# One more stage in the pipeline of latent attention, and two groups of loads sent later

## The chip, the cores and the metric

One core of a Trainium2 chip runs the whole kernel. The time is that of one execution on the device, in microseconds (us), and the median of several runs is compared. Smaller is better.

## The reference

The kernel is one inference step of a two-layer streaming encoder for 576 tokens: 512 of a prompt (SEQ) and 64 of a stream that is continued (DEC), which has a cache of 256 past keys. Both have a width of 1024 (D). Each layer is a half-step feed-forward (width 2816), a mixer, and a second half-step feed-forward. Every sub-layer is modulated by a conditioning vector c and followed by a LayerNorm:

```python
mod = (silu(c) @ w_ada[l] + b_ada[l]).reshape(B, 3, 3, 1, D_MODEL)
shift, scale, gate = mod[:, :, 0], mod[:, :, 1], 1.0 + mod[:, :, 2]
h = swiglu(x * (1.0 + scale[:, 0]) + shift[:, 0], w_ff_in[l, 0], w_ff_out[l, 0])
x = layer_norm(DEEP_ALPHA * x + 0.5 * gate[:, 0] * h, ln_g[l, 0], ln_b[l, 0])
```

The first layer's mixer holds four gated-delta heads and four heads of latent attention, side by side. The attention is this, in blocks of 128 queries, with keys visible by chunks of 64:

```python
s = (einsum('bqhd,bkhd->bhqk', q_nope, k_nope) + einsum('bqhr,bkr->bhqk', q_rope, k_rope)) * MLA_SCALE
p = softmax(where(visible, s, -inf), axis=-1)
out = einsum('bhqk,bkhd->bqhd', p, v)
```

All is in float32. The second layer's mixer is a diagonal state-space layer.

## The kernel before, in words

**The whole.** Each engine has its own program, and semaphores (s_...) order them. TensorE (PE) multiplies tiles of 128 features by 288 tokens. A float32 product is made of three products of rounded parts (hi by hi, hi by lo, lo by hi; `three`, L268). Weights come in blocks of 1 MB or less through a ring of three buffers on SyncE's (SP) DMA queue (`stream_load`, L244); ScalarE (ACT) makes the hi part of a block (`split_hi`, L252) and VectorE (DVE) the lo part (`split_lo`, L259). Activations are split in the same way: ACT makes u_f and u_hi (L538, L542), GpSimd (POOL) makes u_lo (L563).

**The start.** Three DMA queues are issued at once. SP: c_col, c_act (both forms of the conditioning vector), then in turn four pieces each of ada_w0 and ada_w1 (1 MB each; the first rows of the modulation weights), then the weight blocks of the first feed-forward. ACT: x (2304 KB), then nine constants, masks (448 KB) and swap (192 KB) the third and fourth of them. POOL: two pieces of 1 MB of ada_w, the modulation weights for the later rows, whose products DVE makes between blocks of the first feed-forward (`ada_unit`, L655). The order of `ada_vector_first` (L679) is: after the silu of c_act (s_ada_c), sixteen products of ada_w1 (two for each of eight tiles, counted in s_mod1), then a wait for all constants (s_cst), then for PE's sum over ada_w0 (`ada_tensor_first`, L665; s_mod0), then the bias, u_scale and u_shift. ACT splits weight blocks 0 and 1 and then modulates x; PE begins the feed-forward (`head`, L321 on, through `half_step`, L280) when a block's lo part and the first u_lo are there.

masks is read by the gated-delta scan (from 657.9 us on), swap by four products of L1622 that turn the rotary parts (861.3 us).

**Latent attention.** It goes over 20 units: four query blocks by four heads, with 128, 256, 384 and 512 keys, then four decode units of 64 queries and 320 keys. For unit n:

- PE, scores: L1634 and L1635 write one bank of PSUM, bank n % 2.
- DVE: for prompt units the mask (L1729), the row maximum (L1730) and its negative (L1731; s_mx).
- ACT: the exponential into pp, with the row sum (L1686; s_sx).
- DVE: reciprocal and normalising of pp (L1737, L1738; s_pn).
- PE: transpose of pp, 128 keys at a time (L1658; s_tp).
- ACT: copy into ppt (L1696, L1698; s_pc).
- PE: product with the values vt (L1647; s_pv). Every four units ACT and DVE take the hi and lo part of the result (L1704, L1744; s_oh, s_ol).

Each engine has one loop over n, written out by hand. Iteration n holds on PE: scores of n, three matmuls whose result nobody reads (`keep_warm`, L291, in iterations 0 to 9), values of n-2, transpose of n-1. On ACT: exponential of n, copy of n-1. On DVE: maximum of n, then normalising of n-1. After the last unit PE waits for s_ol and begins the output projection (mix_out, L273).

Of the kernel before, what the change touches and what calls it, by code (L numbers as in the profile page):

```python
# [19 lines left out]
ALU = mybir.AluOpType  # L20
# [67 lines left out]
N_CONST = 9 + 1  # L88
# [24 lines left out]
def trunk(nc, i, o):  # L113
# [86 lines left out]
    s_ada_c = sem("conditioning_ready")  # L200
    s_ada_t = sem("modulation_tile_summed")
# [580 lines left out]
    ck_hi, ck_lo = (rt3(n, [P, KPAD], F32R) for n in ("ck_hi", "ck_lo"))  # L782
    rtmp = rt3("rtmp", [P, TOKENS])
    pp = rt3("pp", [P, 2, 512])
# [522 lines left out]
    def gdn_vector(dve):  # L1307
# [71 lines left out]

        dve.wait_ge(s_blk, g_mla)  # L1380
# [195 lines left out]
    NU = len(UNITS)  # L1576

# [10 lines left out]
    def mla_tensor(pe):  # L1588
# [29 lines left out]
        pe.wait_ge(s_evac, g_mla + 2)  # L1618
        for n_, (w, src) in enumerate(((swap[:, 0, :], qr[:, 0, :]), (swap[:, 0, :], qr[:, 1, :]),
                                       (swap[0:64, 1, :], misc[0:64, :]), (swap[0:64, 2, :], misc[0:64, :]))):  # L1620
            for a in range(2):
                mm = pe.matmul(pair(n_)[:, a, :], w, halves(src)[:, a, :], start=True, stop=True)  # L1622
            mm.then_inc(s_rp, 1)
# [3 lines left out]
        for n in range(NU + 2):  # L1627
            if n < NU:
                h, q0, nq, k0, nk = UNITS[n]
                p0 = (h % 2) * 64  # L1630
                if n >= 2:
                    pe.wait_ge(s_sx, n - 1)
                out = ps[0:nq, n % 2, 0:nk]
# [3 lines left out]
            if n < 10:  # L1637
                keep_warm(pe, 6, 3)
            if 2 <= n:
                u = n - 2  # L1640
                h, q0, nq, k0, nk = UNITS[u]
# [8 lines left out]
            if 1 <= n <= NU:  # L1650
                u = n - 1
                h, q0, nq, k0, nk = UNITS[u]
                pe.wait_ge(s_pn, u + 1)
                if u >= 2:
                    pe.wait_ge(s_pc, u - 1)
                for t in range(-(-nk // P)):
                    w = min(P, nk - t * P)
                    mm = pe.transpose(ps[0:w, 2 + u % 2, t * P:t * P + nq], pp[0:nq, u % 2, t * P:t * P + w],  # L1658
                                      ident[0:nq, 0:nq])
                mm.then_inc(s_tp, 1)  # L1660

    def mla_scalar(act):
# [17 lines left out]
        for n in range(NU + 2):  # L1680
            if n < NU:
                h, q0, nq, k0, nk = UNITS[n]
                act.wait_ge(s_mx, n + 1)
                if n >= 2:
                    act.wait_ge(s_tp, n - 1)
                act.activation(pp[0:nq, n % 2, 0:nk], ps[0:nq, n % 2, 0:nk], ACT.Exp, bias=sm[0:nq, 1, n:n + 1],  # L1686
                               scale=MLA_SCALE, accum_out=sm[0:nq, 2, n:n + 1]).then_inc(s_sx, 1)
            if 1 <= n <= NU:
                u = n - 1
# [10 lines left out]
            if n >= 2 and n % 4 == 1:  # L1700
                h, q0, nq, k0, nk = UNITS[n - 2]
                gi = (n - 2) // 4
                act.wait_ge(s_pv, n - 1)
# [4 lines left out]
    def mla_vector(dve):  # L1708
# [14 lines left out]
        for n in range(NU + 2):  # L1723
            if n < NU:
                h, q0, nq, k0, nk = UNITS[n]
                dve.wait_ge(s_sc, n + 1)
                if q0 < SEQ:

                    link(dve.memset(ps[0:CH, n % 2, nk - CH:nk], -1e30))  # L1729
                link(dve.tensor_reduce(sm[0:nq, 0, n:n + 1], ps[0:nq, n % 2, 0:nk], AX.X, ALU.max))  # L1730
                dve.tensor_scalar(sm[0:nq, 1, n:n + 1], sm[0:nq, 0, n:n + 1], -MLA_SCALE, None,  # L1731
                                  ALU.mult).then_inc(s_mx, 1)
            if 1 <= n <= NU:
# [4 lines left out]
                dve.tensor_scalar(pp[0:nq, u % 2, 0:nk], pp[0:nq, u % 2, 0:nk], sm[0:nq, 3, u:u + 1], None,  # L1738
                                  ALU.mult).then_inc(s_pn, 1)
            if n >= 2 and n % 4 == 1:  # L1740
                h, q0, nq, k0, nk = UNITS[n - 2]
                gi = (n - 2) // 4
# [529 lines left out]
    def s5_tensor(pe):  # L2272
# [102 lines left out]
        for b in range(1, 4):  # L2375
            product(pe, "glu", b, 2, KD, u_hi, u_lo)
        out_tensor(pe, "s5_out", 4, KD, glu_hi, lambda k: h_lo[:, k, :], lambda k: pe.wait_ge(s_gl, k + 1))
    constant_loads = [(ident[:, :], i["ident"]), (mean_w[:, :], i["mean_w"]), (masks[:, :, :], i["masks"]),
                      (swap[:, :, :], i["swap"]), (onecol[:, :], i["onecol"]), (b_ada[:, :, :], i["b_ada"]),
                      (ln_g[:, :, :], i["ln_g"]), (ln_b[:, :, :], i["ln_b"]), (cols[:, :], i["cols"])]  # L2380
# [16 lines left out]
    def _(pool):  # L2397
        ada_load(pool, 0, UNITS0, 0)
        u_gpsimd(pool, 0)
# [203 lines left out]
```

## Time and profile before

| | |
|---|---|
| median of 3 runs | 2555.35 us (2549.14 to 2561.02) |
| profiled execution | 2571.54 us, its span 2569.9 us |
| PE busy | 2466.7 us, 96% of the span |
| DVE, ACT, POOL busy | 1453.2, 722.2, 142.5 us |
| mean granted TensorE clock | 0.980 |
| HBM read, written | 259.13 MB, 13.32 MB |

Busy time of PE is the sum of its matmul records, whose ends are modelled. A granted clock of 1.00 is 2.4 GHz, 0.50 is 1.2 GHz. The profiled execution is a single one, 16 us above the median of the timed runs, so differences are worked out within it and then set against the median.

### The profile page before, as it was taken

To read this page: it belongs to the slowest core of one execution; us is meant where nothing else is said; L and a number is where in the kernel's file an instruction comes from. 1 tells how busy PE (TensorE), PEld (TensorE's weight loads), DVE (VectorE), ACT (ScalarE), POOL (GpSimd) and SP (SyncE) were. 2 spreads that over 40 slices of the span, in tenths; PEclk is the share of its full clock that TensorE was granted. 3 is DMA by queue.
4 is the path that set the end of the run, shared out by engine and by line. 5 is a ranking of instruction groups with operands and counts; after the bars stand their busy time and mean duration, and the time that the engine had idled before them with its cause. 6 is when DMAs were issued, how large, how long until landed. Compare 5 with 4: busy or idle time off the path is not lost.

```text
span 2569.9 us, 41177 instructions
## 1 busy us (share of the span) xinstructions
PE 2466.7 (96%) x18104; PEld 2366.9 (92%) x18104; DVE 1453.2 (57%) x2311; ACT 722.2 (28%) x1002; POOL 142.5 (6%) x215
## 2 busy tenths in 40 slices
PE   6999999999899989999999999999989999999996
PEld 6999999998787668999999999999968989999995
DVE  4767765574563435864465686677667455333323
ACT  3211121444333324311121521221255243111212
POOL 2000000200000001100000200000000010000001
PEclk9999999999997889999999999999989999999998
DMA  6445542122000012443343154333324122222221
GB/s 281 150 161 185 183 166 96 64 90 49 13 1 17 27 66 74 159 162 116 122 164 121 61 180 156 111 144 145 140 74 138 58 74 83 78 83 86 83 72 48
DMA packets 55873, 275.09 MB, mean 107 GB/s; under 512 B 7216, under 2 KB 17008, under 8 KB 33040
## 3 DMA queue, kind: packets, MB, share of 16 engines
q1 hardware_dynamic: 38304, 177.43, 19.7%
q0 software_dynamic: 15952, 91.73, 10.1%
q8 instruction: 142, 2.33, 0.4%
q10 hardware_dynamic: 1440, 3.32, 0.4%
q14 instruction: 35, 0.29, 0.0%
HBM read 259.13 MB, written 13.32 MB: 106 GB/s over the span
## 4 chain that ended last, share of the span: by engine, by line
PE 66%; DVE 5%; ACT 1%; issue 1%; DMA 0%; POOL 0%; SPq 0%; DVEq 0%; ACTq 0%
PE ps L273 50%; PE ps L280 4%; PE ps L497 2%; PE ps L480 2%; DVE x L599 1%; PE ps L291 1%; PE ps L1200 1%; PE ps L1209 1%; DVE ln_rstd_tail L595 1%; PE ps L1635 1%; PE ps L1213 0%; PE ps L2338 0%; PE ps L1429 0%; PE ps L1634 0%; PE ps L1420 0%
## 5 line engine op out<-in xcount | busy, mean ns | idle before, releaser
L273 PE MATMUL ps<-u_hi,w_hi 128*128 128x288 f32 x3040 | 653.2, 296 | 2.1 <-DVE w_lo L265 1.2
L273 PE MATMUL ps<-u_hi,w_lo 128*128 128x288 f32 x3040 | 650.3, 296 | 0.0
L273 PE MATMUL ps<-u_lo,w_hi 128*128 128x288 f32 x3040 | 650.3, 296 | 0.0
L265 DVE TENSOR_TENSOR w_lo<-w_raw,w_hi 128x2048 fp32r<-128x2048 f32 (+3 forms) x184 | 360.6, 1960 | 350.0 <-ACT w_hi L257 346.3
L257 ACT ACTIVATE w_hi<-w_raw 128x2048 fp32r<-128x2048 f32 (+3 forms) x184 | 303.5, 1649 | 888.8 <-DMA w_raw<-in_w_in 420.1
L273 PEld LDWEIGHTS ps<-u_hi,w_hi 128*128 128x128 f32 x3040 | 490.7, 189 | 6.8 <-issue 3.5
L273 PEld LDWEIGHTS ps<-u_lo,w_hi 128*128 128x128 f32 x3040 | 490.5, 189 | 0.0
L273 PEld LDWEIGHTS ps<-u_hi,w_lo 128*128 128x128 f32 x3040 | 490.1, 189 | 0.0
L621 DVE SCALAR_TENSOR_TENSOR ada_out<-ada_w,c_act 128x1024 f32<-128x1024 f32 x272 | 317.0, 1221 | 28.8 <-DMA ada_w<-in_w_ada 26.9
L273 PE MATMUL ps<-h_lo,w_hi 128*128 128x288 f32 x1392 | 293.4, 295 | 0.0
L273 PE MATMUL ps<-h_hi,w_hi 128*128 128x288 f32 x1296 | 280.9, 298 | 0.0
L273 PE MATMUL ps<-h_hi,w_lo 128*128 128x288 f32 x1296 | 276.7, 295 | 0.0
L423 DVE TENSOR_TENSOR hf<-ps,sg 128x576 f32<-128x576 f32 x88 | 66.6, 757 | 305.3 <-ACT sg L406 305.3
L273 PEld LDWEIGHTS ps<-h_lo,w_hi 128*128 128x128 f32 x1392 | 222.3, 188 | 0.0
L273 PEld LDWEIGHTS ps<-h_hi,w_hi 128*128 128x128 f32 x1296 | 209.6, 188 | 2.1
L273 PEld LDWEIGHTS ps<-h_hi,w_lo 128*128 128x128 f32 x1296 | 208.3, 188 | 0.0
L406 ACT ACTIVATE sg<-ps 128x576 f32<-128x576 f32 x88 | 57.2, 650 | 491.5 <-PE ps L273 483.1
L449 DVE SCALAR_TENSOR_TENSOR x<-ps,res_gate,x 128x224 f32<-128x224 f32 (+2 forms) x240 | 85.9, 412 | 109.7 <-PE ps L273 85.7
L280 PE MATMUL ps<-u_hi,w_hi 128*128 128x288 f32 x352 | 109.0, 310 | 7.9 <-POOL u_lo L563 7.9
L280 PE MATMUL ps<-u_lo,w_hi 128*128 128x288 f32 x352 | 104.5, 297 | 0.0
L280 PE MATMUL ps<-u_hi,w_lo 128*128 128x288 f32 x352 | 104.3, 296 | 0.0
L563 POOL TENSOR_TENSOR u_lo<-u_f,u_hi 128x288 fp32r<-128x288 f32 x80 | 70.9, 901 | 432.8 <-ACT u_hi L542 431.0
(384 smaller groups left out, 2604.0 us busy)
## 6 DMA issues: line engine op xcount, KB each, us to landing
w_raw<-in_w_in SPq DMA_DIRECT2D x88, 1024.0 KB, 4.8
ada_w<-in_w_ada POOLq DMA_DIRECT2D x64, 1024.0 KB, 4.9
w_raw<-in_w_out SPq DMA_DIRECT2D x32, 768.0 KB, 4.4
w_raw<-in_w_out SPq DMA_DIRECT2D x32, 640.0 KB, 3.8
w_raw<-in_w_mix_in SPq DMA_DIRECT2D x10, 1024.0 KB, 4.9
ada_w<-in_w_ada SPq DMA_DIRECT2D x8, 1024.0 KB, 26.1
output_matrices<-wm_new POOLq DMA_DIRECT2D x8, 576.0 KB, 3.1
wm<-output_matrices POOLq DMA_DIRECT2D x8, 576.0 KB, 4.4
```

What stands on the lines that cost most here:

```text
L257: act.activation(w_hi[:, g % NS, 0:WIDTH[g]], w_raw[:, g % NS, 0:WIDTH[g]], ACT.Copy).then_inc(s_whi, 1)
L265: dve.tensor_tensor(w_lo[:, g % NS, 0:WIDTH[g]], w_raw[:, g % NS, 0:WIDTH[g]], w_hi[:, g % NS, 0:WIDTH[g]].bitcast(F32), ALU.subtract).the ...
L273: m = pe.matmul(out[:, a, :], w, mv[:, a, :], start=start and n_ == 0, stop=stop and n_ == 2)
L280: m = pe.matmul(out, w, mv, start=start and n_ == 0, stop=stop and n_ == 2)
L291: pe.matmul(ps[:, bank_, :], w[:, 0:P], w[:, P:P + 512], start=True, stop=True)
L406: act.activation(halves(sg[:, b % 2, :]), pair(2 * (b % 2)), ACT.Silu).then_inc(s_sg, 1)
L423: dve.tensor_tensor(halves(hf[:, b % 2, :]), pair(2 * (b % 2) + 1), halves(sg[:, b % 2, :]), ALU.mult).then_inc(s_evac, 1)
L449: return dve.scalar_tensor_tensor(out=x[:, b, lo:hi], in0=pair(2 * (b % 2))[:, a, lo - a * HALF:hi - a * HALF], scalar=res_gate[:, site, b ...
L480: return pe.matmul(pair(1)[:, a, :], mean_w[:, :], half(x, k, a), start=k == 0, stop=k == KD - 1)
L497: pe.matmul(pair(3)[:, a, :], mean_w[:, :], sq[:, k % SQ, :], start=k == 0, stop=k == KD - 1).then_inc(s_var, 1)
L563: pool.tensor_tensor(half(u_lo, k, a), half(u_f32, k, a), half(u_hi, k, a).bitcast(F32), ALU.subtract).then_inc(s_up, 1)
L621: return dve.scalar_tensor_tensor(out=ada_out[:, n % 2, :], in0=w, scalar=1.0, in1=c_act[:, st, :], op0=ALU.mult, op1=ALU.mult, accum_out= ...
```

## The change

1. **Loads at the start.** masks and swap leave ACT's list of constants (nine become seven, so s_cst counts eight loads with x). POOL first waits until DVE has made 14 of the sixteen products of ada_w1, then issues its first two pieces of ada_w and after them masks and swap, which count on a semaphore of their own, s_late. DVE waits for s_late before the scan, PE before L1622.
2. **The attention loop.** Scores go through three banks (0, 1 and 6) and pp has three buffers; the first of them lies on rtmp's place, which is no longer needed then. PE's iteration n is now: scores of n, warming matmuls, transpose of n-2, values of n-3. ACT copies n-2; DVE still normalises n-1. The loops have one more iteration, and the u_hi and u_lo pairs move one iteration later.
3. **Warming matmuls.** Two in iterations 0 to 7, in bank 7, in place of three in iterations 0 to 9, in bank 6.

```diff
-N_CONST = 9 + 1
+N_CONST = 7 + 1
...
+    PP0 = rt3.at
     rtmp = rt3("rtmp", [P, TOKENS])
-    pp = rt3("pp", [P, 2, 512])
+    rt3.at = PP0
+    pp = rt3("pp", [P, 3, 512])
...
+        dve.wait_ge(s_late, 32)
         dve.wait_ge(s_blk, g_mla)
...
+    SCORE_BANK = (0, 1, 6)
+    def score(n, rows_, a, b):
+        return ps[0:rows_, SCORE_BANK[n % 3], a:b]
...
+        pe.wait_ge(s_late, 32)
...
-        for n in range(NU + 2):
+        for n in range(NU + 3):
             if n < NU:
-                if n >= 2:
-                    pe.wait_ge(s_sx, n - 1)
-                out = ps[0:nq, n % 2, 0:nk]
+                if n >= 3:
+                    pe.wait_ge(s_sx, n - 2)
+                out = score(n, nq, 0, nk)
...
-            if n < 10:
-                keep_warm(pe, 6, 3)
-            if 2 <= n:
+            if n < 8:
+                keep_warm(pe, 7, 2)
+            if 2 <= n < NU + 2:
                 u = n - 2
+                h, q0, nq, k0, nk = UNITS[u]
+                pe.wait_ge(s_pn, u + 1)
+                if u >= 2:
+                    pe.wait_ge(s_pc, u - 1)
+                for t in range(-(-nk // P)):
+                    w = min(P, nk - t * P)
+                    mm = pe.transpose(ps[0:w, 2 + u % 2, t * P:t * P + nq], pp[0:nq, u % 3, t * P:t * P + w],
+                                      ident[0:nq, 0:nq])
+                mm.then_inc(s_tp, 1)
+            if n >= 3:
+                u = n - 3
                 h, q0, nq, k0, nk = UNITS[u]
                 pe.wait_ge(s_pc, u + 1)
...
-            if 1 <= n <= NU:
-                u = n - 1
-                h, q0, nq, k0, nk = UNITS[u]
-                pe.wait_ge(s_pn, u + 1)
...
-                if n >= 2:
-                    act.wait_ge(s_tp, n - 1)
-                act.activation(pp[0:nq, n % 2, 0:nk], ps[0:nq, n % 2, 0:nk], ACT.Exp, bias=sm[0:nq, 1, n:n + 1],
+                if n >= 3:
+                    act.wait_ge(s_tp, n - 2)
+                act.activation(pp[0:nq, n % 3, 0:nk], score(n, nq, 0, nk), ACT.Exp, bias=sm[0:nq, 1, n:n + 1],
                                scale=MLA_SCALE, accum_out=sm[0:nq, 2, n:n + 1]).then_inc(s_sx, 1)
-            if 1 <= n <= NU:
-                u = n - 1
+            if 2 <= n < NU + 2:
+                u = n - 2
...
-            if n >= 2 and n % 4 == 1:
+            if n >= 3 and n % 4 == 2:
...
-    constant_loads = [(ident[:, :], i["ident"]), (mean_w[:, :], i["mean_w"]), (masks[:, :, :], i["masks"]),
-                      (swap[:, :, :], i["swap"]), (onecol[:, :], i["onecol"]), (b_ada[:, :, :], i["b_ada"]),
-                      (ln_g[:, :, :], i["ln_g"]), (ln_b[:, :, :], i["ln_b"]), (cols[:, :], i["cols"])]
+    constant_loads = [(ident[:, :], i["ident"]), (mean_w[:, :], i["mean_w"]), (onecol[:, :], i["onecol"]),
+                      (b_ada[:, :, :], i["b_ada"]), (ln_g[:, :, :], i["ln_g"]), (ln_b[:, :, :], i["ln_b"]),
+                      (cols[:, :], i["cols"])]
...
     def _(pool):
+        pool.wait_ge(s_mod1, 2 * KD - 2)
         ada_load(pool, 0, UNITS0, 0)
+        pool.dma_start(masks[:, :, :], i["masks"]).then_inc(s_late, 16)
+        pool.dma_start(swap[:, :, :], i["swap"]).then_inc(s_late, 16)
         u_gpsimd(pool, 0)
```

## Rows read from the trace of the kernel before

**Rows 1.** Page, part 4: shares of the chain that ended last, by engine.
```profile
...
PE 66%; DVE 5%; ACT 1%; issue 1%; DMA 0%; POOL 0%; SPq 0%; DVEq 0%; ACTq 0%
...
```

**Rows 2.** Timeline, 0 to 52 us: start us, us, engine, line, operation [idle before <-releaser].
```profile
...
1.41 1.22 POOL L648 DMA_DIRECT2D ada_w<-in_w_ada  x2 [0.83 <-POOLq L2595]
...
15.29 1.89 ACT L637 ACTIVATE c_act<-c_act 128x2048 f32<-128x2048 f32 x1
...
20.11 27.44 PE L671 MATMUL ps<-c_col,ada_w 128*128 128x2 f32 x128 [20.11 <-DMA ada_w<-in_w_ada]
...
40.88 1.23 DVE L621 SCALAR_TENSOR_TENSOR ada_out<-ada_w,c_act 128x1024 f32<-128x1024 f32 x1 [1.67 <-DMA ada_w<-in_w_ada]
...
45.91 1.91 ACT L257 ACTIVATE w_hi<-w_raw 128x2048 fp32r<-128x2048 f32 x1 [0.56 <-DMA w_raw<-in_w_in]
47.69 0.17 DVE L677 TENSOR_TENSOR mod<-ps,b_ada_sb 128x16 f32<-128x16 f32 x1 [2.13 <-PE ps L671]
...
51.54 0.58 PE L280 MATMUL ps<-u_hi,w_hi 128*128 128x288 f32 x1 [3.98 <-POOL u_lo L563]
...
```

**Rows 3.** DMA queues, 0 to 20 us: packets, MB, share of 16 engines.
```profile
...
q0 software_dynamic: 288, 2.10, 24.9%
...
```

**Rows 4.** Windows: us, PE, PEld, DVE, ACT, POOL busy, PEclk, DMA share, GB/s.
```profile
...
16.00:20.00 4.00, 0.00 (x0) 0.00 (x0) 0.00 (x0) 1.18 (x1) 0.00 (x0) 1.00 1.02 424
...
```

**Rows 5.** DMA issues, 0 to 90 us: queue, count, KB each, us to landing.
```profile
...
masks<-in_masks ACTq DMA_DIRECT2D x1, 448.0 KB, 22.6
...
```

**Rows 6.** Timeline of TensorE in latent attention.
```profile
...
870.57 0.49 PE L1634 MATMUL ps<-kn,qn 128*128 128x128 f32 x2 [1.28 <-DVE kr L1722]
...
886.17 0.60 PE L1634 MATMUL ps<-kn,qn 128*128 128x256 f32 x2
...
887.32 0.97 PE L291 MATMUL ps<-w_hi 128*128 128x512 f32 x3
888.13 0.60 PE L1647 MATMUL ps<-ppt,vt 128*128 128x128 f32 x4
...
919.04 0.66 PE L1658 MATMUL ps<-ident,pp 128*128 128x128 f32 x4 [0.67 <-DVE pp L1738]
919.53 1.02 PE L1634 MATMUL ps<-kn,qn 128*128 128x512 f32 x2
...
921.54 1.16 PE L1647 MATMUL ps<-ppt,vt 128*128 128x128 f32 x8
923.36 0.66 PE L1658 MATMUL ps<-ident,pp 128*128 128x128 f32 x4 [0.67 <-DVE pp L1738]
923.95 0.75 PE L1634 MATMUL ps<-kn,qn 128*64 128x320 f32 x2
...
925.31 1.16 PE L1647 MATMUL ps<-ppt,vt 128*128 128x128 f32 x8
...
942.91 0.85 PE L273 MATMUL ps<-u_hi,w_hi 128*128 128x288 f32 x2 [0.93 <-DVE u_lo L1744]
...
```

**Rows 7.** Timelines of VectorE, then ScalarE, for one unit of 512 keys.
```profile
...
921.69 0.11 DVE L1729 MEMSET ps<- 64x64 f32 x1 [2.71 <-PE ps L1635]
...
922.82 0.49 DVE L1738 TENSOR_SCALAR pp<-pp,sm 128x512 f32<-128x512 f32 x1
...
922.75 0.69 ACT L1686 ACTIVATE pp<-ps,sm 128x512 f32<-128x512 f32 x1 [2.42 <-DVE sm L1731]
...
924.05 0.60 ACT L1696 ACTIVATE ppt<-ps 128x512 f32<-128x512 f32 x1 [0.53 <-PE ps L1658]
...
```

**Rows 8.** Waits, 870 to 942 us: waiter <- releaser: us in total, times, longest.
```profile
...
PE ps L1658 <- DVE pp L1738: 6.6, 13, 0.9
...
```

**Rows 9.** Windows in latent attention; columns as in rows 4.
```profile
...
870.50:882.00 11.50, 11.44 (x40) 8.36 (x41) 3.37 (x20) 2.66 (x11) 0.54 (x1) 0.70 0.06 14
898.00:915.00 17.00, 13.51 (x61) 7.30 (x60) 7.14 (x25) 6.02 (x15) 0.00 (x0) 1.00 0.00 1
935.00:942.00 7.00, 6.05 (x25) 4.81 (x24) 1.61 (x6) 1.37 (x6) 0.00 (x0) 0.50 0.01 2
...
```

More of the change, by code:

```diff
@@ L200, in trunk @@
     s_ada_c = sem("conditioning_ready")
+    s_late = sem("late_constants_loaded")
     s_ada_t = sem("modulation_tile_summed")
@@ L1649, in mla_tensor @@
                 mm.then_inc(s_pv, 1)
-            if 1 <= n <= NU:
-                u = n - 1
-                h, q0, nq, k0, nk = UNITS[u]
-                pe.wait_ge(s_pn, u + 1)
[L1654 to L1660, printed above, removed]
     def mla_scalar(act):
@@ L1679, in mla_scalar @@
         split_hi(act, g_mla + 3)
-        for n in range(NU + 2):
+        for n in range(NU + 3):
             if n < NU:
@@ L1699, in mla_scalar @@
                 ins.then_inc(s_pc, 1)
-            if n >= 2 and n % 4 == 1:
-                h, q0, nq, k0, nk = UNITS[n - 2]
-                gi = (n - 2) // 4
-                act.wait_ge(s_pv, n - 1)
+            if n >= 3 and n % 4 == 2:
+                h, q0, nq, k0, nk = UNITS[n - 3]
+                gi = (n - 3) // 4
+                act.wait_ge(s_pv, n - 2)
                 act.activation(u_hi[:, 4:8, q0:q0 + nq],
@@ L1722, in mla_vector @@
         dve.tensor_tensor(kr[:, 0:TOKENS], kr[:, 0:TOKENS], rtmp[:, :], ALU.add).then_inc(s_kr, 1)
-        for n in range(NU + 2):
+        for n in range(NU + 3):
             if n < NU:
@@ L1727, in mla_vector @@
                 if q0 < SEQ:
-                    link(dve.memset(ps[0:CH, n % 2, nk - CH:nk], -1e30))
-                link(dve.tensor_reduce(sm[0:nq, 0, n:n + 1], ps[0:nq, n % 2, 0:nk], AX.X, ALU.max))
+                    link(dve.memset(score(n, CH, nk - CH, nk), -1e30))
+                link(dve.tensor_reduce(sm[0:nq, 0, n:n + 1], score(n, nq, 0, nk), AX.X, ALU.max))
                 dve.tensor_scalar(sm[0:nq, 1, n:n + 1], sm[0:nq, 0, n:n + 1], -MLA_SCALE, None,
@@ L1737, in mla_vector @@
                 link(dve.reciprocal(sm[0:nq, 3, u:u + 1], sm[0:nq, 2, u:u + 1]))
-                dve.tensor_scalar(pp[0:nq, u % 2, 0:nk], pp[0:nq, u % 2, 0:nk], sm[0:nq, 3, u:u + 1], None,
+                dve.tensor_scalar(pp[0:nq, u % 3, 0:nk], pp[0:nq, u % 3, 0:nk], sm[0:nq, 3, u:u + 1], None,
                                   ALU.mult).then_inc(s_pn, 1)
-            if n >= 2 and n % 4 == 1:
-                h, q0, nq, k0, nk = UNITS[n - 2]
-                gi = (n - 2) // 4
+            if n >= 3 and n % 4 == 2:
+                h, q0, nq, k0, nk = UNITS[n - 3]
+                gi = (n - 3) // 4
                 dve.wait_ge(s_oh, 4 + gi + 1)
```

## The prediction

> **What bounds the kernel now.** I read the page first: the chain of work that ended last is 66% TensorE (PE) [rows 1], and elsewhere it jumps between engines. So a change pays where PE starts late or waits. I looked for PE's idle time in the two stretches that the diff touches, with the timeline, the DMA queues, the waits and the granted clock.
>
> *The start.* In [rows 2] PE's first instruction is the 128-column product of L671 at 20.11 us, released by the first piece of ada_w0. From there it runs 27.44 us without a gap: 214 ns for each of 128 matmuls, a rate that later pieces don't hold up. VectorE (DVE) waits for its end at 47.69, modulates, splits the first weight block, and the first real matmul (L280) starts at 51.54. Before 20 us PE only waits for bytes: the DMA engines are full (share 1.02, 424 GB/s) [rows 4], and of what they moved by then 2.10 MB belongs to POOL's queue [rows 3]. Those are the two ada_w pieces issued at 1.41, which the FFN's first blocks use, after 64 us.
>
> *Latent attention.* The first score matmul is at 870.57, the first matmul of mix_out at 942.91 [rows 6]: 72.34 us for 20 units. In a unit of 512 keys the loop is closed through DVE: transposes of the last unit start at 919.04, scores at 919.53, the value product at 921.54; meanwhile DVE masks and takes the maximum from 921.69, and only then normalises the unit before, 922.82 to 923.31 [rows 7]; the next transpose starts at 923.36 [rows 6]. That is 4.32 us, with PE idle 0.67 us by the record and a little more, because a matmul's recorded end runs past the start of one that could follow. Over the stage this wait is 6.6 us in 13 places [rows 8]. ScalarE (ACT) is not the limit: exponential and copy take 0.69 and 0.60 us of the 4.32 [rows 7].
>
> **The change at the start.** POOL's first two loads (2.10 MB) and the masks and swap constants (0.46 and 0.20 MB; [rows 5] has the larger) now go out only after the 14th of DVE's sixteen modulation products. On a full DMA 2.10 MB take 2.10/0.42 = 5.0 us. All of it lies ahead of PE's start; the two constants mostly landed after it (masks 22.6 us after issue), so they relieve later pieces only. PE's start moves from 20.1 to 15.1. The silu of c_act, the other condition, ended at 15.29 + 1.89 = 17.18 [rows 2]; c_act is queued ahead of ada_w0 on SP and also comes earlier, since POOL's queue was sharing with it. A piece of 1.05 MB needs 2.5 us on a free DMA, so c_act lands near 12.5 and its silu ends near 14.5: enough, with little to spare. The 27.44 us follow, so DVE's bias step, and all behind it, come 5.0 us earlier.
>
> What is late next? The last ada_w1 piece, at 40.88 before, now lands some 2.75/0.42 = 6.6 us earlier, at 34.3; two products of 1.2 us later, near 36.7, POOL issues its four transfers (about 1.2 us for the first two [rows 2]; its next task, u_lo, is 8 us off). Weight block 0, next on SP's queue, has landed 2.5 us after that piece, at 36.8. Block 1 (45.91 before) would land at 39.3 alone. ACT splits it (1.91 us) before it may modulate, and modulation can start at 43.3, so block 1 has 2.1 us of slack. If POOL's data halve its rate for its last microsecond or two it is 1 to 2 us late: hidden. If all 2.10 MB went ahead of it, it would be 5.0 late, 2.9 on the path. The new waits on the late constants (DVE before the scan at 650 us, PE before L1622) have been met for hundreds of microseconds: nothing. Start: **-5.0 us**, bounds -2 (that collision) and -6.6 (every deferred byte counts).
>
> The Trainium skill ("DMA: Bandwidth & Descriptors", Queues, rings and completion order) says that each DMA engine goes round the queues packet by packet. By that rule block 1 gets half the rate while POOL's data flow, at worst 2.5 us late, 0.4 on the path; no row shows that collision.
>
> **The change in latent attention.** Per iteration PE did scores n, values n-2, transpose n-1; now it does scores n, transpose n-2, values n-3. Normalising n-2 is finished an iteration earlier, so the transpose waits for nothing; scores n needs the exponential of n-3; the value product needs a copy that ACT made one iteration before. One more iteration drains the pipe. So PE alone sets the pace, and I add its work, start to start [rows 6]:
> - scores: 512 keys 2.01 (919.53 to 921.54), 256 keys 1.15 (886.17 to 887.32), decode 1.36; 384 and 128 by the same slope 1.58 and 0.72. Four each: 27.3.
> - transposes: 0.49 for four tiles, 0.12 a tile, 52 tiles: 6.4.
> - values: four records busy 0.60, eight 1.16, so 0.14 a record, 104 records: 14.6.
> - warming matmuls: three take 0.81; now 2 in 8 iterations, 16 of 0.27 instead of 30: 4.3.
>
> Sum 52.6 us at full clock. To this come: the slow stretch at the front, where 11.5 us had a mean grant of 0.70 [rows 9], that is 6.9 us at half speed, in which PE work takes nearly twice its time: 3.3. The drain, where the last unit's exponential, normalisation, two copies and the u_hi/u_lo pair are exposed: 1.5. And a slow end: before, all of 935 to 942 was at 0.50 (1.2 GHz) [rows 9], with the end-to-end value products at 1.2 GHz; I take 2, between 0 (the clock holds) and 4 (all of the last units). Together 59.4, against 72.34: **-12.9 us**. Half of the gain comes out of waits, 4 us out of fewer warming matmuls. Bounds: -9, if moving between score, transpose and value products costs 0.2 us a unit that the rows hide; -17, if both slow stretches shrink.
>
> Do ACT and DVE keep pace? DVE's work for a unit of 512 keys ran from 921.69 to 923.31, 1.6 us; ACT's is 0.69 and 0.60 and a short readout between them [rows 7]. PE's new period is 3.6. The u_hi and u_lo of each fourth unit follow the value product of n-3 and stand on ACT and DVE ahead of the next maximum; they run beside the next score product, and PE doesn't take that unit's transpose until two iterations on. All of it is covered; uncovered, the pair would cost about one pass of 0.7 us four times.
>
> The edit most open to attack is the smaller number of warming matmuls. In [rows 9] PE had no such matmuls from 898 to 915, was busy 13.51 of 17.00 us, and kept a grant of 1.00; the new loop is denser than that. So I give the removal no price. The Trainium skill ("TensorE: Matmul & The Clock Gate", The HAM clock gate) says the opposite default: throttled unless activity releases it. Taken alone it would keep the front of the stage at 1.2 GHz; the row at 898 speaks against it for the rest.
>
> **Sum.** 5.0 + 12.9 = 17.9 us. The profiled execution took 2571.54 (span 2569.9), so it becomes 2553.6; the timed runs have a median 16 us lower, 2555.35, and from it the same saving gives **2537.4 us**, 0.7% less. A difference under 0.5%, 12.8 us, is about what a measurement can't tell from none.
>
> **Rivals.**
> - *Only the start pays* (0.10). The waits on DVE turn into waits on ACT: exponential, copy and u_hi in one queue. For: the chain touches all of them. Against: ACT's 1.5 us or so per unit [rows 7]. Then attention gives only the warming matmuls and a few waits, 5 us: 2545.
> - *Only attention pays* (0.07). PE's start is set by c_act and its silu, or by x ahead of it on the other queue, or block 1 is late: start -1 to -2, total 14: 2541.
> - *Both clocks hold* (0.10). No slow end in attention and none at the start of mix_out: 22 to 25 us, 2531.
> - *The clock falls and stays down* (0.04), the one that ends slower. With 14 fewer warming matmuls the front of the attention never gets back to 2.4 GHz. Each microsecond of the loop spent at half clock costs 0.4 to 0.5 us; 18 us of gain are eaten by 40 more slow microseconds, and if all 52.6 us of work run slow it is +23 - 18 + 3 = 8 us slower: 2563. For: the clock did fall at the front. Against: the same loop, less dense, held it at 898.
> - *The change does nothing at either place* (0.02): 2555.
> - The forecast itself (0.67): 2531 to 2543 for its own bounds.
>
> Range 2527 to 2547 us: it leaves out the slow-clock case, part of the case of only the start, and some scatter of the median on either side. Faster by over 0.5% needs 12.8 us: forecast, held clocks and most of the second rival, less scatter, 0.80; within 0.5%: 0.16; slower 0.04.
>
> **What the changed profile would show.** PE's L671 group starts near 15 and still lasts 27.4 us; the first L280 matmul starts near 46.5; DVE finds block 0 split; ACT's second split ends before 43. If block 1 is late, ACT's u_f follows that split directly. In attention the transposes wait for nothing on DVE, periods at 512 keys are 3.5 to 3.6 us, and the stage lasts 59 us. I am wrong if PE's idle before the transposes is replaced by idle before value products or scores (ACT as releaser), if PE's first start stays after 18 us, or if the granted clock is at 0.5 for more than some 15 us of the stage.

## The result, and the profile after

| | before | after |
|---|---|---|
| median of 11 runs | 2553.81 us | 2533.02 us |
| lowest to highest | 2535.28 to 2561.69 | 2517.7 to 2544.32 |
| ratio, 95% interval | | 0.9923, 0.9899 to 0.9946 |
| profiled execution, its span | 2571.54, 2569.9 us | 2528.1, 2526.4 us |

By the ratio the change saves 19.7 us (13.8 to 25.8); forecast were 17.9. The whole interval lies beyond 0.5%. Ratios here are those of the fast executions alone: in the session of the first four experiments five of 35 executions of the kernel before (2571 to 8041 us) and one of loop_warm30 (4827 us) are left out of them.

The two spans differ by 43.5 us, over twice what the medians do, so a difference of two profiles must be split before it is read. By the starts of the stages: the first feed-forward begins 5.2 us earlier; from there to the first product of the gated-delta scan 4.0 us are given back; from the scan to the attention it is 11.7 us less, because before had 27.3 us of it at a granted clock of 0.50, from 804.6 us on (before_again, the same kernel profiled once more, lacks that stretch and takes 9.9 us less there); the attention is 19.7 us shorter; the last feed-forward and what follows it are 10.7 us shorter, without an edit there (last section); the rest is 0.2. Only the first and the fourth answer to the edits.

The page after: busy time of each engine, the chain of work that ended last, and the DMA issues of ada_w on SP's queue.

```profile
...
PE 2435.6 (96%) x18090; PEld 2343.1 (93%) x18090; DVE 1453.6 (58%) x2311; ACT 719.6 (28%) x1002; POOL 143.6 (6%) x217
...
PE 66%; DVE 5%; ACT 1%; issue 1%; DMA 0%; POOL 0%; SPq 0%; DVEq 0%; ACTq 0%
...
ada_w<-in_w_ada SPq DMA_DIRECT2D x8, 1024.0 KB, 20.3
...
```

The shares of the chain are those of [rows 1]: the page doesn't show a gain of 0.8%. The stages do. First the start, as a timeline like [rows 2]:

```profile
...
12.22 1.89 ACT L638 ACTIVATE c_act<-c_act 128x2048 f32<-128x2048 f32 x1
...
14.95 27.44 PE L672 MATMUL ps<-c_col,ada_w 128*128 128x2 f32 x128 [14.95 <-DMA ada_w<-in_w_ada]
...
33.01 1.23 DVE L622 SCALAR_TENSOR_TENSOR ada_out<-ada_w,c_act 128x1024 f32<-128x1024 f32 x1 [0.36 <-DMA ada_w<-in_w_ada]
...
35.69 1.22 POOL L649 DMA_DIRECT2D ada_w<-in_w_ada  x2 [35.11 <-DVE ada_out L622]
...
39.52 1.91 ACT L258 ACTIVATE w_hi<-w_raw 128x2048 fp32r<-128x2048 f32 x1 [0.56 <-DMA w_raw<-in_w_in]
42.52 0.17 DVE L678 TENSOR_TENSOR mod<-ps,b_ada_sb 128x16 f32<-128x16 f32 x1 [4.84 <-PE ps L672]
...
46.37 0.58 PE L281 MATMUL ps<-u_hi,w_hi 128*128 128x288 f32 x1 [3.98 <-POOL u_lo L564]
...
```

PE's first product lasts 27.44 us as before and starts at 14.95, not 20.11. DVE's bias step follows at 42.52 (was 47.69), the first real matmul at 46.37 (was 51.54): each 5.2 us earlier. The split of block 1 starts at 39.52 and is over at 41.43, before the bias step. The idle time of DVE ahead of that step has grown from 2.13 to 4.84 us: DVE has more slack and PE alone sets the start. That the 5 us hold further on shows at the tail of the first feed-forward: its first product on L281 comes at 460.51, on L280 before at 465.64.

TensorE's timeline in the attention, the counterpart of [rows 6]:

```profile
...
857.67 0.49 PE L1644 MATMUL ps<-kn,qn 128*128 128x128 f32 x2 [1.25 <-DVE kr L1732]
...
884.77 1.02 PE L1644 MATMUL ps<-kn,qn 128*128 128x512 f32 x2
...
887.16 0.83 PE L1668 MATMUL ps<-ppt,vt 128*128 128x128 f32 x6
887.83 1.02 PE L1644 MATMUL ps<-kn,qn 128*128 128x512 f32 x2
...
891.00 1.02 PE L1644 MATMUL ps<-kn,qn 128*128 128x512 f32 x2
891.96 1.12 PE L1645 MATMUL ps<-kr,qr 64*128 64x512 f32 x2
893.01 0.66 PE L1657 MATMUL ps<-ident,pp 128*128 128x128 f32 x4
893.50 1.06 PE L1668 MATMUL ps<-ppt,vt 128*128 128x128 f32 x8
894.49 0.75 PE L1644 MATMUL ps<-kn,qn 128*64 128x320 f32 x2
...
907.18 2.23 PE L1668 MATMUL ps<-ppt,vt 128*128 128x64 f32 x12
910.34 0.85 PE L274 MATMUL ps<-u_hi,w_hi 128*128 128x288 f32 x2 [0.93 <-DVE u_lo L1754]
...
```

An iteration now mixes three units, so its length depends on all three. One iteration has scores, transposes and value products of 512 keys alone: 891.00 to 894.49, 3.49 us, against 4.32 for the same work before. (884.77 to 887.83 is 3.06 us, but its transposes and values are of 384 keys.) No transpose has a wait in brackets. The stage lasts 857.67 to 910.34, 52.67 us, against 72.34. The waits of the stage (columns as in [rows 8]) say the same: the line of 6.6 us in 13 places is gone, and what is left on PE inside the stage is its first wait, here with the two largest waits of the other engines, of which DVE's is for PE:

```profile
...
ACT pp L1696 <- DVE sm L1741: 35.4, 20, 8.7
...
DVE ps L1739 <- PE ps L1645: 11.7, 13, 1.5
...
PE ps L1644 <- DVE kr L1732: 1.2, 1, 1.2
...
```

ACT's wait for the maximum is long, but nothing on PE waits for ACT.

Three windows, columns as in [rows 4]: the front, the middle and the last units.

```profile
...
857.50:869.00 11.50, 11.33 (x51) 7.62 (x52) 5.72 (x31) 3.63 (x16) 0.54 (x1) 1.00 0.07 14
...
885.00:902.00 17.00, 17.00 (x83) 9.09 (x82) 8.27 (x26) 7.45 (x19) 0.00 (x0) 1.00 0.01 1
...
903.00:910.00 7.00, 6.37 (x38) 4.42 (x37) 2.43 (x8) 2.89 (x13) 0.00 (x0) 0.91 0.00 1
...
```

PE is busy for 17.00 of 17 us in the middle, and the granted clock is 1.00 at the front, where it was 0.70 [rows 9], and 0.91 at the end, where it was 0.50: it fell at 908.7 us, 1.6 us ahead of mix_out, whose first 5 us still ran at 1.2 GHz.

**Where the 19.7 us of the stage come from.** I summed PE's timeline from the start of each group to the start of the next, by kind of product, so that a wait counts with the group ahead of it:

| us | before | after | forecast for after |
|---|---|---|---|
| scores | 28.97 | 27.46 | 27.3 |
| warming matmuls | 9.50 (30) | 4.56 (16) | 4.3 |
| transposes | 8.16 | 6.25 | 6.4 |
| values, with the waits and the drain behind them | 25.71 | 14.40 | 14.6 + 1.5 |
| slow front, slow end | in the rows above | in the rows above | 3.3 + 2 |
| stage | 72.34 | 52.67 | 59.4 |

More than half of the difference, 11.3 us, is the idle time behind the value products and their 1.2 GHz; 4.9 are warming matmuls. This is a comparison of two profiles with different clocks: the slow front, which after lacks, is spread over all rows of before. The experiments take that apart.

### The profile page after: what moved, and what is told of

Same layout as the page of the kernel before. It is cut to its first block, busy times and chain, and to the rows that moved or that the text cites. A ratio compares the mean times of both kernels' runs of the same rounds, so it can differ in the third digit from the quotient of the medians.

```text
span 2526.4 us, 41150 instructions
## 1 busy us (share of the span) xinstructions
PE 2435.6 (96%) x18090; PEld 2343.1 (93%) x18090; DVE 1453.6 (58%) x2311; ACT 719.6 (28%) x1002; POOL 143.6 (6%) x217
## 4 chain that ended last, share of the span: by engine, by line
PE 66%; DVE 5%; ACT 1%; issue 1%; DMA 0%; POOL 0%; SPq 0%; DVEq 0%; ACTq 0%
PE ps L274 50%; PE ps L281 4%; PE ps L498 2%; PE ps L481 2%; DVE x L600 1%; PE ps L1203 1%; PE ps L1212 1%; PE ps L1645 1%; PE ps L292 1%; DVE ln_rstd_tail L596 1%; PE ps L1668 1%; PE ps L1216 1%; PE ps L1644 0%; PE ps L2348 0%; DVE cm L1353 0%
## 5 line engine op out<-in xcount | busy, mean ns | idle before, releaser
L281 PE MATMUL ps<-u_hi,w_hi 128*128 128x288 f32 x352 | 109.0, 310 | 8.0 <-POOL u_lo L564 8.0
L281 PE MATMUL ps<-u_lo,w_hi 128*128 128x288 f32 x352 | 104.5, 297 | 0.0
L281 PE MATMUL ps<-u_hi,w_lo 128*128 128x288 f32 x352 | 104.4, 297 | 0.0
```

The costliest lines, as they stand in the source:

```text
L281: m = pe.matmul(out, w, mv, start=start and n_ == 0, stop=stop and n_ == 2)
```

## The experiments

The stage below is always measured from the first score matmul to the first matmul of mix_out, in one profile of each kernel. A time is given with its ratio to the kernel before, where there is one.

### The two parts apart

loads_only is the kernel before with the change's part 1 and nothing else. loop_only is the changed kernel without part 1:

```diff
-N_CONST = 7 + 1
+N_CONST = 9 + 1
...
-        pool.wait_ge(s_mod1, 2 * KD - 2)
         ada_load(pool, 0, UNITS0, 0)
-        pool.dma_start(masks[:, :, :], i["masks"]).then_inc(s_late, 16)
-        pool.dma_start(swap[:, :, :], i["swap"]).then_inc(s_late, 16)
```

> Only the loads are moved (POOL's two pieces, masks, swap); the attention loop is the old one. Theory of bytes ahead: TensorE's first sum starts at 15 us instead of 20.1, the first feed-forward matmul at 46.4, and nothing of it is given back: 5 us less in the time. Rival, something later in the first feed-forward or before the scan waits for the late pieces and gives part of it back: the first matmul at 46.4, but less than 3 us left at the first matmul of mix_in. In attention the stage lasts 72 us as before, give or take the clock.

> Only the attention loop is changed; the loads are the old ones. Theory: the stage from the first score matmul to the first matmul of mix_out lasts 52 to 56 us instead of 72, transposes wait for nothing, the time is 13 to 19 us less. With the run of the loads alone the savings add up to that of both (about 20). Rival, the shorter stage was luck of the clock in one profile: the stage lasts 59 us or more here and the gain is under 13.

Measured: loads_only 2555.60 us, ratio 0.9993 (0.9962 to 1.0023); PE starts at 15.1 and the feed-forward at 46.5, as after; its attention takes 71.3 us. loop_only 2542.58 us, ratio 0.9941 (0.9916 to 0.9967); PE starts at 20.4, the feed-forward at 51.8, the attention takes 52.6 us. In the stages that they touch the parts are independent. In the times the loop's part is 15 us, as expected (13 to 19), and that of the loads 1.8 us with an interval from 9.7 gained to 5.9 lost: the 5 us at the start are seen in the trace and can't be confirmed by this measurement.

### Depth, buffers, or fewer warming matmuls

warm_only is the kernel before with 16 warming matmuls for 30. banks_only has the loads, the three banks and buffers and the 16 warming matmuls of the changed kernel, but the old depth and order.

```diff
# warm_only, against before
-            if n < 10:
-                keep_warm(pe, 6, 3)
+            if n < 8:
+                keep_warm(pe, 6, 2)
```

```diff
# banks_only, against the changed kernel (PE; ACT and DVE likewise)
-        for n in range(NU + 3):
+        for n in range(NU + 2):
...
-            if 2 <= n < NU + 2:      # transpose of n-2, then values of n-3
+            if 2 <= n:               # values of n-2, then transpose of n-1
```

> The kernel before with only the number of warming matmuls cut, two in iterations 0 to 7. In the old loop transposes wait for VectorE in most iterations, so most of the cut ones lay in that wait. Theory: the stage gets at most 1 to 2 us shorter and the time can't be told from before. Rival, fewer of them take the array to 1.2 GHz for longer: the stage at 0.50 for more than the 7 us at its front, 75 us or more in all.

> The loads and the number of warming matmuls as in the changed kernel, three score banks and three probability buffers, but the old order and depth of the loop (transpose of n-1 after values of n-2). Theory: the wait is on the normalising of the unit just before, which more buffers don't bring forward: transposes wait 6 us or more in all and the stage lasts 68 to 71 us. Rival, the buffers alone free the loop: the stage lasts under 60 us.

Measured: warm_only 2556.46 us, ratio 0.9997 (0.9970 to 1.0024), stage 68.7 us. banks_only 2523.17 us in one run, stage 68.8 us. A wait and a part of the timeline of banks_only:

```profile
...
PE ps L1668 <- DVE pp L1748: 10.3, 18, 0.9
...
```

```profile
...
887.96 1.02 PE L1644 MATMUL ps<-kn,qn 128*128 128x512 f32 x2
888.92 1.12 PE L1645 MATMUL ps<-kr,qr 64*128 64x512 f32 x2
889.97 1.16 PE L1657 MATMUL ps<-ppt,vt 128*128 128x128 f32 x8
891.80 0.66 PE L1668 MATMUL ps<-ident,pp 128*128 128x128 f32 x4 [0.67 <-DVE pp L1748]
892.29 1.02 PE L1644 MATMUL ps<-kn,qn 128*128 128x512 f32 x2
...
```

With three banks and the old order the period is still 887.96 to 892.29, 4.33 us, and the transposes wait 10.3 us in 18 places. So the buffers alone give nothing (68.8 us against 68.7 for warm_only) and the depth gives it all; they are what the depth needs. banks_only and the changed kernel have the same loads, buffers and warming matmuls and both held the clock at the front: 68.79 against 52.67, so the order and depth are worth 16.1 us, and the 19.7 of the two first profiles contain 3.6 more.

Those 3.6 are not the warming matmuls. The two old-order kernels with 16 of them take 68.7 to 68.8 us, the three profiles with 30 (before, before_again, loads_only) 71.3 to 72.3; but these three had a slow front of 6.8 us and the two had none. Summed as in the table, warm_only against before_again has 4.1 us less in warming matmuls and 1.3 less in scores, and 2.9 more in values with the waits behind them. At full clock 30 warming matmuls take 8.05 us (loop_warm30, below), not 9.36, so 1.3 of the 4.1 and the 1.3 of the scores are the clock, and what the 14 matmuls cost, 2.8, comes back as wait for DVE: in the old loop they lay in waits, as expected. That banks_only's one time is 10 us below the median of the changed kernel, with an attention stage 16 us longer, shows what a single time is worth.

### The warming matmuls in the new loop

My prediction gave their removal no price. Three kernels try other numbers: three in ten iterations (loop_warm30), one in eight (warm_one), none (no_warm).

```diff
# loop_warm30, against loop_only
-            if n < 8:
-                keep_warm(pe, 7, 2)
+            if n < 10:
+                keep_warm(pe, 7, 3)
```

> The changed kernel with the old number of warming matmuls, three in iterations 0 to 9 (in bank 7). Theory: in the new loop TensorE sets the pace, so each of the 14 extra matmuls costs its 0.27 to 0.29 us: 4 us slower than the changed kernel, the stage at 56 to 57 us at full clock. Rival, they lie in waits: same time. Rival of the clock: with them the front of the stage holds 2.4 GHz more surely and the time is the same or less.

> The changed kernel with no warming matmuls inside the attention loop. Theory: TensorE sets the pace in the new loop, so the 16 cost 0.27 us each; without them the stage lasts 48 to 49 us instead of 52.6, at a granted clock of 1.00 up to the last units, 4 us less in the time. Rival of the clock: without them the array falls to 1.2 GHz in the units of 128 and 256 keys, the granted clock there reads 0.50, and the stage is as long as with them or longer (53 us or more).

> The changed kernel with one warming matmul instead of two in iterations 0 to 7. Without any the array was at 1.2 GHz for 20.5 us in the attention loop and the stage took 58.2 us; with two it held 2.4 GHz until the last units and took 52.6. Theory, the activity of one is enough: 50.4 us. Rival, it is not: a stretch at 0.50 in the units of 128 and 256 keys, 54 us or more.

loop_warm30 is built on loop_only, with the old loads, whatever its expectation names; it is compared with loop_only. Its stage is 55.9 us against 52.6: 14 matmuls cost 3.4 us, 0.24 each, and the granted clock was 1.00 in both. Its time, 2550.17 us, ratio 0.9990 (0.9959 to 1.0020), is 7.6 us above loop_only's; the trace accounts for 3.4 of them. One thing doesn't fit: its interval allows at most 10.5 us of gain over the kernel before, and its stage is 15.5 us shorter than before_again's. In its profile nothing is given back elsewhere (last section), so the times and the trace differ here, and why stays open.

With fewer than two the clock fell, and stayed down for long. Windows of no_warm, then of warm_one, over the slow stretch, columns as in [rows 4]:

```profile
...
859.40:886.00 26.60, 26.22 (x78) 14.83 (x79) 10.97 (x50) 7.69 (x29) 0.55 (x1) 0.62 0.03 6
...
```

```profile
...
855.00:878.00 23.00, 22.80 (x71) 14.03 (x72) 9.24 (x43) 5.81 (x23) 0.55 (x1) 0.63 0.03 7
...
```

no_warm had 20.5 us at 1.2 GHz and a stage of 58.2 us; warm_one 17.1 us and 58.6 us. A stage at full clock without the warming matmuls would be 52.67 - 4.56 = 48.1, so 20.5 slow microseconds cost 10.1; with one each it would be 50.4, so 17.1 cost 8.2: 0.49 and 0.48 us for each slow microsecond. PE was busy 26.22 of 26.60 us there by its records, and still the clock stayed down for most of it. My argument from the row at 898 [rows 9] doesn't carry over to the first units, which are short. The Trainium skill ("TensorE: Matmul & The Clock Gate", The HAM clock gate) calls the throttled state the default from which activity releases. These two runs agree in part: with fewer matmuls the clock came back later, but records that are busy throughout didn't bring it back for 20.5 us.

Whether the clock falls at all isn't shown to hang on the number. Some 20 to 25 us ahead of the stage every profile has a stretch at 0.50. Where it lasted 6.8 us (eight profiles) the clock fell again 2 to 3 us into the stage in six: before, before_again, loads_only, after_again, no_warm, warm_one, and not in late_on_act and x_middle. Where it lasted 3.4 us (six profiles: after, loop_only, loop_warm30, warm_only, banks_only, x_last) it held. What differs with the number is how long it stayed down: 6.8 us in all four with two or three matmuls an iteration (three of them in the old order), 17.1 with one, 20.5 with none, the last two in one profile each.

In times: no_warm 2534.19 us, ratio 0.9925 (0.9895 to 0.9955), level with the changed kernel; warm_one 2544.71 us in one run. The 5.5 us by which no_warm's stage is longer are too few to show.

### The same two kernels again

after_again and before_again are the changed kernel and the kernel before, unedited, for a second profile of each.

> The changed kernel once more, for what repeats between two profiles. Theory: first sum at 14.9 to 15.6 us, attention 52 to 53 us at full clock nearly to its end. The feed-forward stages may each fall 9 us one way or the other, as they did in other runs. If the clock of the first profile was luck, the stage is 56 us or more here.

> The kernel before once more. Theory: first sum at 20 to 21 us, attention between 68 and 72.5 us, by how long the array is at 1.2 GHz at the front of the stage (7 us in the first profile, none in the kernel with only fewer warming matmuls, 68.7). If 72.3 was bad luck, the part of the gain that the change earns is nearer to 16 us than to 20.

Windows of after_again, then before_again, at the front of the attention:

```profile
...
858.80:870.40 11.60, 11.51 (x40) 8.08 (x41) 4.38 (x24) 3.03 (x13) 0.55 (x1) 0.71 0.06 14
...
```

```profile
...
864.00:876.00 12.00, 11.88 (x41) 8.51 (x42) 3.65 (x21) 2.67 (x11) 0.55 (x1) 0.72 0.06 14
...
```

Times 2542.12 and 2544.07 us, stages 56.3 and 71.4. The second profile of the changed kernel had the slow front that the first lacked: 6.8 us at 1.2 GHz, 3.6 us more. Of six profiles of the new loop with two warming matmuls, five held the clock there (after, loop_only, x_last, late_on_act, x_middle) and this one didn't. So the forecast's 3.3 us for it was a cost that comes in some executions, and 52.7 us is the better case of the stage, not its only one. Slow front against slow front the loop saves 71.4 - 56.3 = 15.1 us, full clock against full clock 16.1.

### What is given back before the scan

From ACT's first write of qkv to the scan's first product the changed kernel took 133.8 us and loads_only 132.9, against 129.3 before. A part of it is one wait of PE for DVE, the first spread of the norms. Timelines of after, loads_only, late_on_act and after_again:

```profile
...
597.27 3.39 PE L1062 MATMUL ps<-rn,ident 8*128 8x288 f32 x8 [1.39 <-DVE rn L1048]
...
```

```profile
...
590.84 4.20 PE L1060 MATMUL ps<-rn,ident 8*128 8x288 f32 x8 [2.21 <-DVE rn L1046]
...
```

```profile
...
598.25 2.20 PE L1062 MATMUL ps<-rn,ident 8*128 8x288 f32 x8 [0.63 <-DVE rn L1048]
...
```

```profile
...
598.43 2.20 PE L1062 MATMUL ps<-rn,ident 8*128 8x288 f32 x8 [0.62 <-DVE rn L1048]
...
```

late_on_act takes the two constants off POOL's queue and issues them from ACT, after its first two splits:

```diff
-        pool.dma_start(masks[:, :, :], i["masks"]).then_inc(s_late, 16)
-        pool.dma_start(swap[:, :, :], i["swap"]).then_inc(s_late, 16)
...
+        act.dma_start(masks[:, :, :], i["masks"]).then_inc(s_late, 16)
+        act.dma_start(swap[:, :, :], i["swap"]).then_inc(s_late, 16)
```

> The changed kernel, but masks and swap are loaded by ScalarE's queue after its split of weight block 1, not by POOL's. In both kernels with the two loads on POOL's queue the store of the small convolution rows landed 1 to 2 us later than in the four with the old loads, and TensorE waited 1.4 to 2.2 us at the first norm spread (about 597 us) instead of 0 to 0.4. Theory, the two extra transfers on POOL's queue do it: here that wait is back at 0 to 0.4 us. Rival, it comes from the time at which the stage is reached or by chance: the wait stays at 1.4 us or more.

Measured 2530.05 us, ratio 0.9899 (0.9855 to 0.9943); wait 0.63 us, between the two expectations; stretch 130.2 us. That looked like a cure, but after_again has the same 0.62 us, with a stretch of 131.2, and the constants on POOL. The run alone decides nothing; all fourteen profiles say more. With the constants late on POOL's queue the stretch takes 128.1 to 133.8 us, mean 131.3 of eight; in the other six it takes 129.3 to 131.3, mean 130.3. The wait is 0.00 to 2.21 us, mean 0.9, against 0.00 to 0.63, mean 0.3. So the deferred loads cost about 1 us there if anything, and the 4 us given back in the first pair of profiles were mostly scatter.

### A later x

At the start PE still waits only for bytes, and now for x, 2304 KB ahead of it on ACT's queue. x is needed at modulation, after 42 us. x_last puts it on SP's queue behind the eight pieces of ada_w, and lets POOL issue after PE's sum. x_middle puts it between weight blocks 0 and 1, and lets ACT and DVE split block 1 after the first modulation:

```diff
# x_last, against the changed kernel
+        sp.dma_start(x[:, :, :], i["x"]).then_inc(s_cst, 16)      # after ada_sync(sp)
...
-        pool.wait_ge(s_mod1, 2 * KD - 2)
+        pool.wait_ge(s_mod0, 1)
...
-        act.dma_start(x[:, :, :], i["x"]).then_inc(s_cst, 16)
```

```diff
# x_middle, beyond that (the x load stands in stream_load, after block 0)
-        for b in range(2):
-            split_hi(act, b)
+            split_hi(act, a)         # one block, then its half of u
...
-        for b in range(2):
-            split_lo(dve, b)
+        split_lo(dve, 0)             # split_lo(dve, 1) after DVE's share of u
```

> The changed kernel with x (2.36 MB) loaded after the modulation pieces instead of first, and POOL's loads after TensorE's sum over ada_w0. Theory of bytes ahead: the first sum starts when c_act's silu is done and one piece has landed, near 9 us instead of 14.9, still lasts 27.4 us, and the first feed-forward matmul starts 4 to 5 us earlier, at 41 to 42.5, held by ScalarE's split of weight block 1. Rival, the sum is then held up by its pieces: it starts earlier but lasts longer than 28 us. Rival, x is late: the first modulation waits for it and the matmul starts at 45 or later.

> On top of the run with x last: x is loaded between weight blocks 0 and 1, ScalarE splits block 1 only after it has modulated the first half of the tokens, and VectorE takes its part of that split last. In the run with x last the modulation (from 38.3 us possible by VectorE's scales) waited for ScalarE's split of block 1 until 40.64. Theory: modulation starts at 37.5, the first feed-forward matmul at 39.7 to 41 instead of 43.9, and the time is some 3 us less than with x last, 6 us less than the changed kernel. Rival, block 1 is now late for TensorE: a wait of more than 1 us before the first matmul of block 1, and the gain is gone at the first matmul of mix_in.

Timeline of x_last, then of x_middle:

```profile
...
9.40 27.43 PE L672 MATMUL ps<-c_col,ada_w 128*128 128x2 f32 x128 [9.40 <-DMA ada_w<-in_w_ada]
...
38.83 1.91 ACT L258 ACTIVATE w_hi<-w_raw 128x2048 fp32r<-128x2048 f32 x1 [0.57 <-DMA w_raw<-in_w_in]
...
40.64 0.61 ACT L539 ACTIVATE u_f<-x,u_shift,u_scale 128x288 f32<-128x288 f32 x1
...
```

```profile
...
37.50 0.63 ACT L541 ACTIVATE u_f<-x,u_shift,u_scale 128x288 f32<-128x288 f32 x1 [4.88 <-DVEq L716]
...
40.72 0.58 PE L283 MATMUL ps<-u_hi,w_hi 128*128 128x288 f32 x1 [3.98 <-POOL u_lo L566]
...
```

PE starts at 9.4 and 9.3, earlier by about the 5.6 us that x's bytes take at 424 GB/s. In x_last only 2.4 us of them reach the feed-forward (43.9, where 41 to 42.5 were expected): the modulation stands behind ACT's split of block 1, which is the late thing now, the case that I had asked about for the change itself. x_middle takes the split out of the way and starts the feed-forward at 40.72, 5.65 us before the changed kernel. Times: x_last 2521.41 us, ratio 0.9876 (0.9833 to 0.9919); x_middle 2524.88 us, ratio 0.9867 (0.9839 to 0.9896). The late block that was the rival to x_middle costs PE no wait above 0.4 us. x_middle is the version that I would keep: the best ratio to before, from four executions. Its interval just misses that of the change (0.9899 to 0.9946), in another session; the two ratios lie 14 us apart, of which the trace explains 5.65. The interval of x_last overlaps that of the change, so that x_last beats it rests on the trace alone.

## Why the prediction was right

- **The start, -5.0: right, step by step.** PE's sum at 14.95 (forecast 15.1), c_act's silu over at 14.11 (14.5), POOL's issue at 35.69 (36.7), block 1 at 39.5 (39.3), first modulation at 43.16 (43.3), first matmul at 46.37 (46.5). PE's start moved by 5.16 us. The collision of POOL's loads with block 1 doesn't show: its split starts 2.48 us behind that of block 0, what a piece takes on a free DMA, and 0.2 us behind the forecast. By the packet rule of the Trainium skill ("DMA: Bandwidth & Descriptors", Queues, rings and completion order) my estimate was 2.5 at worst; nothing here tests the rule, since the two hardly met: POOL's queue had moved 0.02 MB by 39 us, and the rest after block 1.
- **The attention's mechanism: right.** Transposes wait for nothing, PE sets the pace, ACT and DVE keep up, and banks_only shows that it is the order and depth, 16.1 us, and not the buffers.
- **The attention's size: too small, -12.9 for -19.7.** In this pair of profiles even my bound of -17 was short; with equal clocks it was 15 to 16. Term by term, 52.67 against 59.4: scores +0.2, transposes -0.15, warming matmuls +0.3. "values: four records busy 0.60, eight 1.16, so 0.14 a record" is the mis-sized term: these are modelled busy times, where the distance from start to start was wanted. Inside a row it is 0.11 us, before too; the row of eight at 921.54 is longer by one distance of 0.21 at its head, which most rows of the new loop lack. Eight of them now take 0.99 start to start, six 0.67. The 92 records before the last group take 11.24 us, 0.122 each, not 12.9. "The slow stretch at the front" (3.3) was absent here and present in after_again, which took 56.3 with it, still 3.1 under the forecast's 59.4. The last 12 records with drain and slow end took 3.16, against 1.7 + 1.5 + 2: the clock fell only in the last two microseconds. Sum: -1.7 - 3.3 - 2.0 and the small ones, -6.7. The period at 512 keys, forecast 3.5 to 3.6, was right where all three units have 512 keys (3.49). The periods just before it, 3.06 to 3.17, have value products of 384 keys, a mixing that my forecast of the period overlooked and its sum, which counts records, did not.
- **"So I give the removal no price": not contradicted for two, wrong as a rule.** I reasoned from a stretch without warming matmuls at 384 and 512 keys to units of 128. no_warm and warm_one had 20.5 and 17.1 us at half clock exactly at the front, where the rival put them. Both lost more to the clock than they saved, 10.1 for 4.6 and 8.2 for 2.3; the rival's full price (all 52.6 us slow) was not reached, since the clock came back by itself in the units of 384 keys and at the end of those of 256.
- **The total.** 17.9 forecast, 19.7 measured. The stages say 5.2 + 15 to 20: with repeats, 71.3 to 72.3 us before and 52.4 to 56.3 after. A sum of 20 to 25 less some 1 us before the scan is in the measured interval, but the agreement with 17.9 is closer than its terms deserve, and in part luck: the separate parts gave 15 and 1.8 us in their session, and the interval of the second includes no gain at all.
- **Rivals.** Only the start, or nothing at either place: excluded by loop_only. Only attention: excluded by the trace at 46.37, though not by the time of loads_only. Both clocks hold: at the front the profile after is that case and after_again is not; at the end neither is, since the clock fell within the last units and mix_out began at 1.2 GHz. The clock falls and stays down: not with two matmuls; with fewer it stayed down longer, and came back.

## What to carry to other kernels

Where PE waits a little in each iteration of a two-deep pipeline, add a stage before you add buffers, and cost the new loop by distances from start to start, not by busy times. Price warming matmuls in the shortest units, not where the loop is dense: where PE waits anyway they are free, and where it sets the pace each costs its time, unless the clock is down. Judge their number by more than one profile, since the same kernel held the clock in one and not in the next. When the first matmul waits for bytes, list what lies in the queues with it and when each is first read: in the traces 2.1 MB off the road were 5 us, and x another 5.6, until a split behind a late block took its place.

## What the hardware did that I had not expected

**Two rates of the same products at the same clock.** A feed-forward's stream of matmuls without a gap ran at one of two speeds for a whole stage. Windows of 100 us in the last feed-forward, of before, before_again, after and loop_only:

```profile
...
2200.00:2300.00 100.00, 100.00 (x752) 100.00 (x751) 31.56 (x36) 17.94 (x14) 0.00 (x0) 1.00 0.21 77
...
```

```profile
...
2200.00:2300.00 100.00, 100.00 (x772) 100.00 (x771) 32.12 (x42) 16.43 (x13) 0.00 (x0) 1.00 0.23 76
...
```

```profile
...
2200.00:2300.00 100.00, 100.00 (x771) 100.00 (x771) 31.48 (x42) 17.70 (x13) 0.00 (x0) 1.00 0.25 85
...
```

```profile
...
2200.00:2300.00 100.00, 100.00 (x752) 100.00 (x751) 30.27 (x40) 16.44 (x13) 0.00 (x0) 1.00 0.22 74
...
```

752 or 771 matmuls in 100 us, 133 or 130 ns each, PE busy throughout and the granted clock 1.00 in all. From its first matmul to the first of its tail the second, third or fourth feed-forward takes 396.7 to 397.0 or 405.4 to 405.7 us; the first takes 405 to 407 or 413 to 416. Of 14 profiles with four feed-forwards each, 24 of 56 stages ran at the faster rate, mixed among all kernels, the one before too. At 9 us a stage this is up to 35 us in a run, more than the change gives, and fits the scatter of one kernel's runs (2535 to 2562 us here); banks_only, with its low time, had all four fast. Its cause is open; no run here aimed at it.

With these four stretches taken out, the spans of the profiles line up much better than the whole times do: before 947.6 us (with its long slow stretch) and before_again 936.2, warm_only 933.2, loads_only 933.0, banks_only 925.1, loop_warm30 920.6, warm_one 919.8, no_warm 918.2, after_again 916.8, loop_only 916.3, late_on_act 913.3, after 913.0, x_last 909.4, x_middle 906.6. The two profiles of the changed kernel still differ by 3.9 us, so this shows the loop's part and a later x, and not the 5 us of the loads for certain.

**The first microseconds run at 1.2 GHz, and the profile doesn't say so.** Lines of the first feed-forward of after, then of the attention of before:

```profile
...
46.98 0.44 PE L281 MATMUL ps<-u_hi,w_lo 128*128 128x288 f32 x1
47.23 0.44 PE L281 MATMUL ps<-u_hi,w_hi 128*128 128x288 f32 x1
...
52.07 0.29 PE L281 MATMUL ps<-u_hi,w_hi 128*128 128x288 f32 x1
52.20 0.30 PE L281 MATMUL ps<-u_lo,w_hi 128*128 128x288 f32 x1
...
```

```profile
...
877.32 0.63 PE L1647 MATMUL ps<-ppt,vt 128*128 128x128 f32 x2
877.74 0.42 PE L1658 MATMUL ps<-ident,pp 128*128 128x128 f32 x1
...
```

Up to 52 us the matmuls of 288 columns start 0.24 us apart, afterwards 0.13. In all fourteen profiles the pace changes within 0.2 us of the first entry on the clock in the trace; the windows before it print 1.00, as in [rows 4], for want of an entry. PE's sum at the start, 27.44 us for 128 matmuls or 214 ns each, has the distance of products with 128 weight columns at a granted clock of 0.50 (877.32 to 877.74, two in 0.42 us; 0.11 each at 1.00). So the 27.44 us on which the start hangs are by this reading at 1.2 GHz. What a PE at 2.4 GHz would give there no run shows; the split of block 1, over at 41.43, would be the next thing to wait for.

**A busy engine at half clock.** In no_warm PE was busy by its records for 26.22 of 26.60 us around the slow stretch, on products of 128 to 384 columns, and was granted 1.2 GHz for 20.5 us of it.
